# A two-layer encoder step on one core: where the second layer's memory projection runs, and how two experts' rows are added

## The reference

```python
for l in range(DEPTH):                      # DEPTH = 2
    if l == 0:
        o_main = mla_attention(...)         # from x @ w_in_a
    else:
        kv = x @ w_kv_shared                # 1024 x 1536, the shared keys and values
        o_main = diff_attention(q_d, kv, ...)
    o_mem = memory_attention(q_m, mem_k[l], mem_v[l])   # mem_prompt @ w_mem_kv[l]: 256 x 1024 by 1024 x 512
    mix = concat([o_main, o_mem]) @ w_out[l]
    x = layernorm(DN_ALPHA * x + mix)
    x = layernorm(DN_ALPHA * x + grouped_moe(x))        # 16 experts of width 512, top 2 of the best group
```

## Time and profile before

| | us |
|---|---|
| median of three runs | 924.26 (921.4 to 925.52) |
| the profiled execution | 930.91 |
| its span | 929.1 |
| PE busy | 804.1 (87%) |
| DVE busy | 335.7 (36%) |
| ACT busy | 186.6 (20%) |
| DMA | 272.82 MB, 294 GB/s over the span |

### The profile page before, as it was taken

One profiled execution on the slowest core, in us unless ns is written; L12 is line 12 of the kernel. 1 busy time (PEld: TensorE's weight loads), 2 busy tenths in 40 slices (PEclk: granted clock), 3 DMA queues, 4 the chain that ended last, 5 costly groups with the idle time before them and its releaser, 6 DMA issues.

```text
span 929.1 us, 10037 instructions
## 1 busy us (share of the span) xinstructions
PE 804.1 (87%) x3983; PEld 399.1 (43%) x3983; DVE 335.7 (36%) x749; ACT 186.6 (20%) x452; POOL 44.0 (5%) x58
## 2 busy tenths in 40 slices
PE   6998999999999887877889988979899998777865
PEld 3665877464433222222334666754534332222221
DVE  1025445435422212122280153545543442112228
ACT  1213343110221101110110035630103211111101
POOL 1012000002000000000100000000030000000020
PEclk9998999888999999998999998979999999999988
DMA  9734007745999999999789060392669999999991
GB/s 356 228 87 174 1 1 284 305 167 206 376 425 426 423 429 423 427 423 424 261 316 373 27 233 1 123 382 84 272 235 421 431 421 428 423 429 421 428 395 55
DMA packets 43553, 272.82 MB, mean 294 GB/s; under 512 B 6360, under 2 KB 11166, under 8 KB 25840
## 3 DMA queue, kind: packets, MB, share of 16 engines
q1 hardware_dynamic: 32032, 243.69, 63.9%
q0 software_dynamic: 5888, 19.95, 6.3%
q10 hardware_dynamic: 5584, 8.51, 2.5%
HBM read 253.92 MB, written 18.21 MB: 293 GB/s over the span
## 4 chain that ended last, share of the span: by engine, by line
PE 55%; DMA 26%; DVE 10%; SPq 6%; ACT 2%; issue 1%; ACTq 0%; POOL 0%; DVEq 0%; POOLq 0%
DMA arena<-in_expert_w_up 24%; PE bank L923 16%; PE bank L865 6%; PE bank L937 5%; PE bank L1183 5%; PE bank L852 3%; SPq L503 2%; PE bank L839 2%; PE bank L688 2%; PE bank L784 2%; PE bank L946 1%; PE bank L681 1%; PE bank L832 1%; PE bank L875 1%; PE bank L762 1%
## 5 line engine op out<-in xcount | busy, mean ns | idle before, releaser
L923 PE MATMUL bank<-arena 128*64 128x512 f32 x1024 | 239.6, 624 | 53.6 <-DMA arena<-in_expert_w_up 51.8
L923 PEld LDWEIGHTS bank<-arena 128*64 128x64 f32 x1024 | 76.8, 144 | 213.3 <-issue 147.0
L937 PE MATMUL bank<-arena 128*64 128x512 f32 x512 | 116.9, 598 | 16.7 <-DVE arena L1832 16.7
L1832 DVE COPY arena<-bank 128x256 f32<-128x256 f32 x32 | 13.6, 424 | 276.1 <-PE bank L930 276.1
L937 PEld LDWEIGHTS bank<-arena 128*64 128x64 f32 x512 | 33.9, 136 | 77.6 <-issue 54.8
L1385 ACT ACTIVATE arena<-bank 128x256 f32<-128x256 f32 x32 | 12.3, 383 | 270.3 <-PE bank L923 270.3
L1840 DVE RECIPROCAL arena<-arena 128x256 f32<-128x256 f32 x32 | 56.1, 1753 | 1.1
L865 PE MATMUL bank<-arena 128*128 128x512 f32 x128 | 56.0, 595 | 0.0
L1183 PE MATMUL bank<-arena 128*128 128x512 f32 x96 | 43.1, 609 | 5.0 <-DVE arena L1530 5.0
L1241 ACT COPY arena<-bank 128x512 f32<-128x512 f32 (+2 forms) x30 | 15.8, 537 | 107.1 <-PE bank L681 70.0
L865 PEld LDWEIGHTS bank<-arena 128*128 128x128 f32 x128 | 24.0, 190 | 29.6 <-issue 29.5
(11 more groups left out here) (272 smaller groups left out, 890.8 us busy)
## 6 DMA issues: line engine op xcount, KB each, us to landing
arena<-in_expert_w_gate SPq DMA_DIRECT2D x32, 2048.0 KB, 22.9
arena<-in_expert_w_up SPq DMA_DIRECT2D x32, 2048.0 KB, 27.9
arena<-in_expert_w_down SPq DMA_DIRECT2D x64, 1024.0 KB, 29.3
arena<-in_w_out SPq DMA_DIRECT2D x4, 2048.0 KB, 9.9
expert_rows<-arena ACTq DMA_DIRECT2D x60, 128.0 KB, 7.9
arena<-in_w_kv_shared SPq DMA_DIRECT2D x3, 2048.0 KB, 10.4
arena<-in_w_mem_kv SPq DMA_DIRECT2D x2, 2048.0 KB, 21.3
arena<-sorted_rows POOLq DMA_DIRECT2D x2, 2048.0 KB, 9.6
```

The source lines that it names most:

```text
L923: last = mm(bank[j][64 * half:64 * half + 64, :].rearrange("p (u f) -> p u f", u=2), slots[:, k, 0:CAP], w[:, :, k, 256 * half:256 * half ...
L937: last = mm(bank[3 + j][64 * n:64 * n + 64, :], hid_t[:, j, c, 64 * half:64 * half + 64], w[:, half, c, 512 * n:512 * n + 512], start=(hal ...
```

## The change

Three things are moved, and a number of loads and copies with them.

First, layer 2's memory projection. The memory features that the start makes for layer 1 are written by POOL to a scratch in DRAM, ahead of its store of `bias_rows`. In layer 1's routing SP reads them back together with `w_mem_kv[1]`, which goes into `dn_one`, the third down buffer. PE does the projection's sixteen products in place of the warming products of layer 1's routing, in pieces of 1, 1, 8, 2, 2 and 2 (`memory_some`, `meanwhile`), in banks 3 and 4. ACT copies the result, SP stores it, and only when it has landed are expert 2's down weights loaded. The keys and values that layer 2's attention needs are read back from the outputs later. POOL's read of the sorted rows waits for the projection.

Second, `PAIR` is true for layer 1 too: experts 14 and 15 stay in SBUF and are added by `add_tile`.

Third, the order behind layer 1's experts. The blocks of `w_kv_shared` are loaded when the downs of experts up to 13 and the ups up to 14 are done. PE adds tiles 0 and 1, turns tile 0 and does its shared keys (`kvs0`), and only then adds tile 2, the sample. DVE and ACT follow: DVE adds the sample's gathered rows behind the copy for `x2a`, and ACT's roots for tiles 1 and 2 stand ahead of its copies for `kvs0`.

```diff
@@ -47,7 +47,7 @@
-PAIR = (False, True)
+PAIR = (True, True)
...
+        feat_dram = nc.dram_tensor("memory_features", (P, KC * MEM), F32, kind="Internal").ap()
...
-        mem_in1 = ring[3][:, 0:2 * D].rearrange("p (t d) -> p t d", t=2)
-        mem_feat1 = ring[3][:, 2 * D:4 * D].rearrange("p (k m) -> p k m", k=KC)
+        w_mem = [ring[i][:, :].rearrange("p (k f) -> p k f", k=KC) for i in (0,)] + [dn_one.rearrange("p (k f) -> p k f", k=KC)]
+        mem_feat1 = Region(xs_at + 2 * D).cut(KC, MEM)
+        mem_new1 = dn_one[:, 0:4 * MW].rearrange("p (t w) -> p t w", t=2)
...
-            return bank[((0, 1), (5, 6), (2, 7))[t][c]]
+            return bank[((0, 1), (3, 4), (2, (0, 7)[l]))[t][c]]
...
                 load_up(l, 1, ups[1], up_in[1])
+                if l == 0:
+                    sp.dma_start(mem_feat1.rearrange("p k m -> p (k m)"), feat_dram).then_inc(feat_in, 16)
+                    load_mem(1)
                 if l == 1:
                     load_down(1, 1, 1, dn_in[1])
                 sp.wait_ge(proj_ready, job_end(before_gu1))
                 load_up(l, 2, ups[2], up_in[2])
+                if l == 0:
+                    sp.wait_ge(mem1_copied, 2)
+                    store_mem(1, mem_new1[:, :, 0:MW], mem_new1[:, :, MW:2 * MW])
+                    sp.wait_ge(out_mem, 64)
                 load_down(l, 2, 2, dn_in[2])
...
                 if l == 0:
+                    sp.wait_ge(down_done, NE - 2)
+                    load_kvs(0)
                     sp.wait_ge(up_done, NE - 1)
-                    sp.dma_start(mem_in1, ins["mem_prompt"][0].rearrange("(t p) d -> p t d", p=P)).then_inc(mem_in_s, 16)
-                    load_mem(1)
+                    for c in (1, 2):
+                        load_kvs(c)
...
             sp.wait_ge(down_done, NE)
-            for t in range(3):
-                sp.wait_ge(back_in[t], 32)
-            load_kvs(0)
-            sp.wait_ge(proj_ready, job_end("memkv1"))
-            for c in (1, 2):
-                load_kvs(c)
...
-            sp.wait_ge(*emptied(job_end("memkv1") - 1))
-            store_mem(1, mem_raw1[:, 0], mem_v1)
-            for dst, src in ((mem_raw1[:, 1], ins["cache_mem_k"][1, 0]), (smem_v1, ins["cache_mem_v"][1, 0])):
+            for dst, src in ((mem_raw1[:, 0], outs["new_mem_k_prompt"][1, 0]), (mem_v1, outs["new_mem_v_prompt"][1, 0]),
+                             (mem_raw1[:, 1], ins["cache_mem_k"][1, 0]), (smem_v1, ins["cache_mem_v"][1, 0])):
...
+            mem_at = [0]
+
+            def memory_some(count):
+
+                for i in range(mem_at[0], mem_at[0] + count):
+                    t, k = divmod(i, KC)
+                    if i == 0:
+                        pe.wait_ge(feat_in, 16)
+                        pe.wait_ge(w_in["mem1"], 16)
+                    last = mm(bank[3 + t][:, :], mem_feat1[:, k, P * t:P * t + P], w_mem[1][:, k, :],
+                              start=k == 0, stop=k == KC - 1)
+                mem_at[0] += count
+                if mem_at[0] == 2 * KC:
+                    last.then_inc(mem1_done, 1)
+
+            def meanwhile(l, columns, count):
+
+                if l == 0:
+                    memory_some(count)
+                else:
+                    keep_warm(bank[1], columns)
...
                 logits(0)
+                if l == 0:
+                    memory_some(1)
                 pe.wait_ge(ln_done, 6 * l + 3)
                 tile_to_features(f"xb{l}", x_tok, 1)
-                keep_warm(bank[1], 512)
+                meanwhile(l, 512, 1)
...
-                keep_warm(bank[1], 2048)
+                meanwhile(l, 2048, 8)
...
-                keep_warm(bank[1], 512)
+                meanwhile(l, 512, 2)
                 for n, who in enumerate("av"):
...
-                keep_warm(bank[1], 512)
+                meanwhile(l, 512, 2)
                 pe.wait_ge(pick_ready, l + 1)
                 pack_first(l)
+                if l == 0:
+                    memory_some(2)
...
-            pe.wait_ge(mem_in_s, 32)
-            memory_features("memx1", mem_in1)
-            pe.wait_ge(w_in["mem1"], 16)
-            for n in range(2):
-                pe.wait_ge(*emptied(job0["memx1"] + 2 + n))
-            memory_kv("memkv1", mem_feat1, w_mem[1])
-
+            for t in range(2):
+                add_tile(0, t)
             for t in range(3):
...
+                if t == 0:
+                    add_tile(0, 2)
                 if t == 1:
-                    pe.wait_ge(mem1_in, 32)
-                    pe.wait_ge(*emptied(job_end("memkv1") - 1))
+                    pe.wait_ge(mem1_in, 64)
...
+            ac.wait_ge(feat_out, 16)
             for k, b in jobs("cqss"):
...
-                        ac.wait_ge(ln_done, 6)
+                        ac.wait_ge(part_ready, 3)
...
+                if l == 0:
+                    ac.wait_ge(mem1_done, 1)
+                    for t in range(2):
+                        nc.scalar.copy(mem_new1[:, t, :], bank[3 + t][:, :]).then_inc(mem1_copied, 1)
                 gate(0)
...
-                if l == 0:
-                    copies("memx1", mem_dst(mem_feat1))
-                memkv1 = jobs("memkv1")
                 for t in range(3):
-                    if l == 0 and t == 2:
+                    if l == 0 and t == 1:
                         copies("x2a", feat_dst)
                     root(2 * l + 1, t)
-                    if l == 0 and t < 2:
-                        k, b = next(memkv1)
-                        own(nc.scalar.copy(mem_raw1[:, 0, k, :], b[:, 0:MW]))
-                        out_of(nc.scalar.copy(mem_v1[:, k, :], b[:, MW:2 * MW]))
...
+                def add_rows(t):
+                    n = TOKS[t][1]
+                    ve.wait_ge(back_in[t], 32 * (l + 1))
+                    for s in range(2):
+                        step(stt(x_tok[0:n, t, :], back[0:n, s, t, :], pair_gate[0:n, s, t:t + 1], x_tok[0:n, t, :],
+                                 ALU.mult, ALU.add), part_ready if s else None)
+
                 if PAIR[l]:
...
+                    add_rows(0)
+                    add_rows(1)
                 combine(0)
                 ln_finish(2 * l + 1, 0)
-                combine(1)
                 if l == 0:
                     copies("x2a", feat_dst)
+                if PAIR[l]:
+                    add_rows(2)
+                combine(1)
                 ln_finish(2 * l + 1, 1)
                 combine(2)
                 ln_finish(2 * l + 1, 2)
...
+            for n in range(2, 4):
+                po.wait_ge(*emptied(job0["memx"] + n))
+            po.wait_ge(w_in["mem0"], 16)
+            po.dma_start(feat_dram, mem_feat_in.rearrange("p k m -> p (k m)")).then_inc(feat_out, 16)
             po.wait_ge(*emptied(job0["bias"]))
...
                 po.wait_ge(x_sorted, 96 * (l + 1))
+                if l == 0:
+                    po.wait_ge(mem1_done, 1)
```

More of the change, by code:

```diff
@@ L1924, in after_attention @@
                 own.settle()
-                if l == 0 and not PAIR[0]:
-                    copies("memx1", mem_dst(mem_feat1))
                 def combine(t):
@@ L1931, in combine @@
                         ve.wait_ge(tile_ready, 3 * pairs(l) + t + 1)
[L1932 removed]
+                        sums = [sum_bank(l, t, c)[0:n, :] for c in range(2)]
                         for c in range(2):
```

29 lines of the change are left out of this document (13 added, 16 removed).

## The result

| | before | after |
|---|---|---|
| median of 6 runs each, us | 923.18 | 937.39 |
| lowest and highest | 918.52, 929.72 | 932.42, 941.96 |
| ratio, 95% interval | | 1.0141 (1.0097 to 1.0184) |
| the profiled execution | 930.91 | 932.42 |
| its span | 929.1 | 929.9 |

The kernel is slower, by 9 to 17 us. Yet the two profiled executions have nearly the same span: the one of before is slower than each of the six runs beside it, the one of after the fastest of its six. Two traces can therefore not be compared by their ends. They can be compared stretch by stretch, between landmarks, and a stretch counts only if it repeats in other traces. That is how the rest of this text reads them.

A forecast was written before the change was run, and what follows sets the result against it. Bounds in turn: small loads, PE and engines around it, DMA bytes, PE again. Terms +2.5 - 0.8 + 5.0 + 1.5 - 5.8 = +2.4 on the profiled 930.91 give 933.3; less 6.7 to the median, 926.7, written 927; range 918 to 937.

The forecast's parts named there:

- within 0.5%: Whole kernel: the time changes by no more than 4.6 us either way; chance 0.43.
- slower: Whole kernel: the time grows by more than 4.6 us; chance 0.40.
- a slow clock in the routing: Layer 1's routing: doubled PE run at 1.2 GHz delays rank by 3.6 to 6.8 us; used for the range's high side.
- a hole at the stores: Layer 1's expert stream: expert 3's loads wait behind the projection's stores; some 3 us in the range's high side.
- start: Kernel start: the feature write delays the bias store and the small loads behind it, +2.5 us (0 to +5).
- routing: Layer 1's routing: sixteen memory products replace PE's warming products ahead of rank, -0.8 us (-2.3 to +7).
- stream, bytes: Layer 1's experts: 2.1 MB of expert 2's down weights enter the full DMA stream at 421 GB/s, +5.0 us.
- stream, hole or later start: Layer 1's experts: loads issued at about 239 instead of 235.75 us, behind the projection's stores, +1.5 us (0 to +5).
- behind T: After layer 1's experts: shared keys end earlier, partly given back by a PE pause before tile 1, -5.8 us (-4.3 to -8).
- T: End of layer 1's last down product: 454.43 us before, forecast near 462.6, 8.2 later.
- the clock stays low: Rival in layer 1's routing: slow PE delays rank by 3.6 to 6.8 us, time 931 to 934; chance 0.33.
- the prediction's own sign: End of layer 1's last down product: if it hardly moves, the stream has slack and the prediction is wrong.

## Why the prediction was right or wrong

The forecast was 927 with a range of 918 to 937, and the likeliest case was "within 0.5%". The time came out at 937.4, at the very edge of the range and 1.0141 times the former, so the likeliest case was wrong and the case "slower", with 0.40, held; but not by the rival that carried most of it. The upper end stood for a slow clock in the routing and a hole at the stores, and neither came; that the range reached as far as the time did is luck.

| term | predicted | measured, by landmarks |
|---|---|---|
| start | +2.5 | +2.5 (62.9 to 65.4, means) |
| routing | -0.8 | +1.1 (9.62 to 10.76 at the full clock) |
| stream, bytes | +5.0 | +4.1 |
| stream, hole or later start | +1.5 | +1.5, cause not shown |
| behind T | -5.8 | -3.5 (69.1 to 65.5, means) |
| layer 2's end | none | +3.7 (20.4 to 24.1) |
| sum | +2.4 | +9.4 |

**The start** was right in place and size: the write moves the last small load by 2.5 us in the means, and not by 0. The Trainium skill's rule (DMA: Bandwidth & Descriptors, Rules for kernel authors), by which the bias store uses at most six of sixteen engines, led to 2.5 us where the mean share alone led to 0; the traces without and with the write, 62.9 and 65.4, agree with the rule, but which engines carry the store no trace here shows.

**The routing** had the wrong base. The prediction took the first trace's 13.1 us, at a granted clock of 0.52, as what the kernel before does, and credited the change with a rise of the clock. At the full clock before takes 9.6 and waits for DVE; sixteen instructions instead of eight outlast that wait. Its 0.82 us an instruction at 1.2 GHz was read too low as well: the run it comes from spans the clock's rise, and the two warming instructions ahead of it, at a granted clock of 0.50, took 0.86 each (204.52 to 206.23 us). The rival "the clock stays low" did not occur in any of the changed kernel's traces at this place: its granted clock was 1.00 between the transposes and rank in all but one, which showed 0.94 and 11.3 us.

**The stream** was right in its main term: the down weights that move into the full stream cost 4.1 us instead of 5.0. The hole did not come: the stores landed in 3.5 us instead of the 6 assumed, and the DMA share was 1.00 again from 228 us on. That what remains is 1.5 too is luck, and its cause stays open. By the prediction's own sign, that it is wrong if T hardly moves, it would have failed: T came at 455.38, 0.95 later than before instead of 8.2. The sign was badly chosen, since it counts from the start of the span: the small load came 3.0 us later, but attention took 5.3 and the routing 2.4 less, and from rank on T came 5.6 later.

**Behind T** the mechanism was right to the wait: T+10.2 for T+9.9, T+41.8 for T+41.0. The term was mis-sized: tile 1's keys took 23.55 and not 22.2, at a granted clock of 0.88 behind the pause where the 22.23 of before had 0.94, and tile 1 started 0.8 later.

**Layer 2's end** was missing. The prediction read the reordered additions as an edit to layer 1 alone, though the function serves both layers, and the diff shows no condition on the layer there. It used layer 2's tail as the model of the new path in layer 1 and did not ask what the new order does to that tail.

**The rest.** The landmarks sum to +9.4; the first series measured +13 (9 to 17), the second +19 (12 to 26) by the ratio and +11 by the medians of all runs. Over all series the 12 runs of after have a mean of 937.4. The kernel before has medians of 923 to 929 in four series of 6 to 19 runs. Against the middle of these, 926 to 927, the difference is some 11. So 9.4 lies at the lower end of what was measured. Whether the rest is a lower clock that the changed kernel's pauses bring, beyond the two places shown, stays open: layer 1's attention differs by up to 8 us between traces of the changed kernel and its variants, and the stretch from the keys' end to T2 lies between 379 and 388 us over all traces, with means of 382.4 in the three of the old kernel and its variant and 385.3 in the nine others.

## What to carry to other kernels

A function that serves two stages is changed in both: look for every caller of a reordered step, and price the order where it was already good. Before a stretch's time becomes the base of a term, ask which clock it ran at, and take the base from a second trace or from the same code elsewhere. A load that moves out of an idle stretch costs its bytes in the full one, and its place in the queues decides what it delays besides.

## What the runs showed of the hardware

A read of 2.4 MB on POOL's queue was held up by loads on SP's queue more than their bytes take at 421 GB/s (5.0 us for 2.1 MB): PE waited 11.25 us for the sorted rows when 2.1 MB of down weights were issued 0.3 us ahead of the read and the next expert's loads followed, 7.87 us with half of those weights 2.8 us ahead, and at most 1.23 us in six traces with all of them 1.6 to 3.4 us behind it. One trace with half of them 1.7 us behind doesn't fit in (2.92 us), and how the two queues share the engines no run here shows. And equal work on PE takes 135.8 to 143.3 us in layer 1's attention from one execution to the next, with mean granted clocks of 0.96 to 0.92, in four traces whose programs are the same up to there.
